# Triangular inverses with products on half the blocks, and another order of work in a mixer's first head

## The reference, cut to what matters

```python
D_MODEL, SEQ, DEPTH, N_HEADS_DN, HEAD_DIM_DN, CHUNK = 1024, 512, 2, 8, 128, 64
SHORT_CONV, DW_WIDTH, D_FF = 4, 31, 2816            # one sequence, float32

def reference(x, ...):
    for l in range(DEPTH):
        x = x + 0.5 * swiglu(rmsnorm(x), w_gate, w_up, w_down)
        x = x + hybrid_mixer(rmsnorm(x), ...)
        x = x + 0.5 * swiglu(rmsnorm(x), ...)
    return rmsnorm(x, final_norm)

def hybrid_mixer(h, ...):
    qkv, g_out, a, b, glu, gates = split(h @ w_in)
    q, k, v = split(silu(causal_depthwise_conv(qkv, taps=4)))      # 8 heads of 128
    beta, g = sigmoid(b), -exp(a_log) * softplus(a + dt_bias)
    o = gated_delta_chunked(l2norm(q) * 128 ** -0.5, l2norm(k), v, g, beta)
    y_a = (rmsnorm(o, head_norm) * silu(g_out)) @ w_a_out
    c = causal_depthwise_conv(val * sigmoid(gt), taps=31) + bias
    y_b = silu(rmsnorm(c)) @ w_b_out
    return (sigmoid(gate_a) * y_a + sigmoid(gate_b) * y_b) @ w_o

def gated_delta_chunked(q, k, v, g, beta):
    m = einsum(kb, k) * decay_strict                # strictly lower triangular
    sol = triangular_solve(eye + m, rhs)            # here: by the inverse of eye + m
    ...
    step: v_new = u - w @ state; o = qd @ state + attn @ v_new; state = state * eg + kd^T @ v_new
```

## Time and profile before

| | us |
|---|---|
| median of 3 runs | 2915.28 |
| lowest, highest | 2908.36, 2915.95 |
| the profiled execution, its own time | 2912.12 |
| its span, first to last instruction | 2910.3 |

### The profile page before, as it was taken

The page is one execution under the profiler, slowest core; times in us unless marked ns, Lnnn a source line. Parts: engine busy times, 40 slices in busy tenths (PEclk is TensorE's granted clock), DMA queues, the critical chain, the costliest instruction groups (busy, mean ns, idle before and its releaser), DMA issues.

```text
span 2910.3 us, 37509 instructions
## 1 busy us (share of the span) xinstructions
PE 2835.3 (97%) x13920; PEld 2365.2 (81%) x13920; DVE 1661.6 (57%) x2465; ACT 1103.3 (38%) x1650; POOL 335.4 (12%) x292
## 2 busy tenths in 40 slices
PE   7999989999999999999999999899999999999999
PEld 6888867888887888888888888688888878888887
DVE  5554346888887345554345543578788853555432
ACT  3322245555554233332322223455465532333221
POOL 1000021211222010000000001211121310200001
PEclk8999999999999999999999999999999999999999
DMA  4333386786664533333333335768867554233332
GB/s 142 101 94 96 90 126 108 108 111 118 112 117 74 110 94 94 94 102 94 96 95 100 94 92 100 128 105 105 120 108 115 116 75 105 87 100 95 94 97 68
DMA packets 479201, 296.80 MB, mean 102 GB/s; under 512 B 12181, under 2 KB 462869, under 8 KB 479093
## 3 DMA queue, kind: packets, MB, share of 16 engines
q1 hardware_dynamic: 462964, 236.63, 38.3%
q0 software_dynamic: 16128, 58.73, 10.5%
HBM read 234.51 MB, written 2.10 MB: 81 GB/s over the span
## 4 chain that ended last, share of the span: by engine, by line
PE 84%; DVE 5%; ACT 5%; DMA 3%; issue 2%; POOL 1%; SPq 0%; POOLq 0%; DVEq 0%; ACTq 0%
PE bank L428 82%; PE bank L565 2%; DMA w_lo<-raw 1%; DMA raw<-in_w_in 1%; DVE cacc L1274 1%; ACT w_hi L781 1%; ACT w_lo L783 1%; ACT NT L926 1%; ACT kd L932 0%; DVE w_lo L1048 0%; DMA prow<-in_qkv_conv_w 0%; DVE XT L1386 0%; DVE mg_lo L1512 0%; ACT thv L922 0%; DVE g_lo L1064 0%
## 5 line engine op out<-in xcount | busy, mean ns | idle before, releaser
L781 ACT ACTIVATE w_hi<-raw 128x1024 fp32r<-128x1024 f32 x448 | 472.3, 1057 | 635.1 <-PE bank L428 614.7
L1048 DVE TENSOR_TENSOR w_lo<-raw,w_hi 128x1024 fp32r<-128x1024 f32 x336 | 412.9, 1229 | 507.6 <-ACT w_hi L781 507.6
L428 PE MATMUL bank<-h_hi,w_hi 128*128 128x512 f32 x1504 | 591.0, 393 | 13.2 <-DVE h_lo L1073 6.0
L428 PE MATMUL bank<-h_lo,w_hi 128*128 128x512 f32 x1504 | 588.5, 391 | 0.0
L428 PE MATMUL bank<-h_hi,w_lo 128*128 128x512 f32 x1504 | 588.4, 391 | 0.0
L1274 DVE SCALAR_TENSOR_TENSOR cacc<-c_raw,ncol,cacc 128x512 f32<-128x512 f32 x464 | 381.1, 821 | 7.8
L428 PE MATMUL bank<-g_lo,w_hi 128*128 128x512 f32 x928 | 380.9, 410 | 0.0
L428 PE MATMUL bank<-g_hi,w_lo 128*128 128x512 f32 x928 | 379.8, 409 | 0.0
L428 PE MATMUL bank<-g_hi,w_hi 128*128 128x512 f32 x928 | 376.5, 406 | 0.0
L428 PEld LDWEIGHTS bank<-h_hi,w_hi 128*128 128x128 f32 x1504 | 284.3, 189 | 74.7 <-issue 10.8
L428 PEld LDWEIGHTS bank<-h_hi,w_lo 128*128 128x128 f32 x1504 | 284.2, 189 | 59.8
(11 more groups left out here) (245 smaller groups left out, 3713.2 us busy)
## 6 DMA issues: line engine op xcount, KB each, us to landing
raw<-in_w_in SPq DMA_DIRECT2D x128, 512.0 KB, 8.7
w_lo<-raw POOLq DMA_DIRECT2D x112, 512.0 KB, 7.0
raw<-in_ffn_w_gate SPq DMA_DIRECT2D x88, 512.0 KB, 3.8
raw<-in_ffn_w_up SPq DMA_DIRECT2D x88, 512.0 KB, 3.8
raw<-in_ffn_w_down SPq DMA_DIRECT2D x64, 512.0 KB, 3.9
raw<-in_ffn_w_down SPq DMA_DIRECT2D x32, 384.0 KB, 3.4
raw<-in_w_a_out SPq DMA_DIRECT2D x16, 512.0 KB, 5.1
raw<-in_w_b_out SPq DMA_DIRECT2D x16, 512.0 KB, 4.1
```

The source lines that it names most:

```text
L428: return nc.tensor.matmul(o, a, b, start=start, stop=stop, **kw)
L781: nc.scalar.activation(w_hi[c % SLOTS][:, :], raw[c % SLOTS][:, :], ACT.Copy).then_inc(hi_done, 1)
L1048: tt(w_lo[c % SLOTS][:, :], raw[c % SLOTS][:, :], w_hi[c % SLOTS][:, :].bitcast(F32), ALU.subtract).then_inc(lo_v, 1)
```

## The change

Three parts.

The inverse: a level's off-diagonal blocks lie in odd rows' blocks and even columns' blocks only. X is now packed: ScalarE copies the odd columns' blocks (XO) and the even ones (XE) of all four chunks out of bank 0, each 256 columns in place of 512. GpSimd packs the odd blocks of NT for each level (n0 to n5, 256 elements). Each small product then serves two chunks at once: y and xy are two products in place of four, the transposes between levels two in place of four. A half-wide product on VectorE (YD) with a mask of diagonal blocks takes the place of the masked copy; xy accumulates into the even blocks of bank 0, which holds X itself; one full copy (XF) and one full transpose (xtf, XTF) follow the last level. On ScalarE dense_steps(0), (1) and (2) now follow halves(1), (3) and (5), and the negatives of two units are moved between levels. On GpSimd deci comes ahead of mean_root, and n0 and n1 too. VectorE has the same lists, with two taps behind the last level.

Round 0: norm_stats after 6 half-stages in place of 12, norm_spread after 13 in place of 18; norm_factor ahead of the work on wab; lo of unit 3, wab_lo and hnh behind scale(0); the k taps before the wait for ScalarE's first exponents, and those ahead of w_hi of unit 2's successor; the sums of g after half-stage 63 and the exponents behind unit 4.

Residues of the first four mixer units by VectorE instead of ScalarE and DMA.

```diff
-PE_ORDER = "H H gr H H kt kk H kq H so H H x2t vt H H y0 fb H H xy0".split()
+PE_ORDER = "H H gr H H kt kk H kq H so H H x2t vt H H xt0 y0 fb H H xy0".split()
 for _l in range(1, LEVELS):
-    PE_ORDER += f"H H H H xt{_l - 1} y{_l} H H H xy{_l}".split()
-PE_ORDER += "H H vn0 H H os0".split()
+    PE_ORDER += ("H H H " if _l < LEVELS - 1 else "H H H H ").split() + f"xt{_l} y{_l} H H H xy{_l}".split()
+PE_ORDER += "H H H xtf H H H vn0 H H os0".split()
...
                     elif name[0] == "y":
                         lv = int(name[1:])
-                        ac("X2")
-                        ac("kd")
-                        if lv:
-                            ve(f"x{lv - 1}")
-                        each(bank[1], NT, X, name)
+                        ac(f"XE{lv}")
+                        pe.wait_ge(po_dn.sem, po_dn.after(rn, f"n{lv}"))
+                        t, at = NO[lv]
+                        for q in range(2):
+                            m = mm(bank[1][:, q * P:q * P + P], t[:, (at * 2 + q) * P:(at * 2 + q + 1) * P], X[:, (2 + q) * P:(3 + q) * P])
+                        m.then_inc(*pe_dn.step(name))
...
                 def xy(lv, rn):
-                    pe.wait_ge(ac_dn.sem, ac_dn.after(rn, f"Y{lv}"))
-                    if lv < LEVELS - 1:
-                        each(bank[2], XT, Y, f"xy{lv}")
-                    else:
-                        each(bank[2], Y, XT, f"xy{lv}")
+                    pe.wait_ge(ac_dn.sem, ac_dn.after(rn, f"XT{lv}"))
+                    pe.wait_ge(ve_dn.sem, ve_dn.after(rn, f"yd{lv}"))
+                    even = alternate(bank[0], lv, 0)
+                    nb = P // (2 << lv)
+                    for q in range(2):
+                        m = mm(even[:, q * nb:q * nb + nb, :], XT[:, q * P:q * P + P], YD[:, q * P:q * P + P].rearrange("p (b s) -> p b s", s=2 << lv),
+                               start=False, stop=True, skip_group_check=True)
+                    m.then_inc(*pe_dn.step(f"xy{lv}"))
...
                             if rn is None:
-                                if s == HALVES:
+                                if s == HALVES // 2:
                                     norm_stats(l * 3 + 1, 2)
-                                elif s == HALVES + HALVES // 2:
+                                elif s == HALVES + 1:
                                     norm_spread(l * 4 + 1, 3)
...
+                                elif s == 5 * HALVES + 3:
+                                    ab_sums()
...
+                    def halves(lv):
+
+                        pe_(f"xy{lv - 1}" if lv else "x2t")
+                        nc.scalar.activation(packed(X, 0, lv), alternate(bank[0], lv, 1), ACT.Copy).then_inc(*ac_dn.step(f"XO{lv}"))
+                        nc.scalar.activation(packed(X, 1, lv), alternate(bank[0], lv, 0), ACT.Copy).then_inc(*ac_dn.step(f"XE{lv}"))
+
+                    def turned(lv):
+
+                        pe_(f"xt{lv}")
+                        nc.scalar.activation(XT[:, 0:2 * P], bank[2][:, 0:2 * P], ACT.Copy).then_inc(*ac_dn.step(f"XT{lv}"))
...
+                    halves(0)
+                    turned(0)
+                    halves(1)
                     dense_steps(0, *dense)
...
+                    turned(1)
+                    hi(Rd, c0 + 4)
+                    halves(2)
+                    turned(2)
+                    negative(c0 + 4)
+                    halves(3)
+                    squares(0, 1)
+                    dense_steps(1, *dense)
+                    turned(3)
+                    hi(Rd, c0 + 5)
+                    halves(4)
+                    turned(4)
+                    negative(c0 + 5)
+                    halves(5)
+                    squares(2, 3)
+                    dense_steps(2, *dense)
+                    turned(5)
+                    hi(Rd, c0 + 6)
...
+                    pe_(f"xy{LEVELS - 1}")
+                    nc.scalar.activation(X[:, :], bank[0][:, :], ACT.Copy).then_inc(*ac_dn.step("XF"))
+                    pe_("xtf")
+                    nc.scalar.activation(XT[:, :], bank[3][:, :], ACT.Copy).then_inc(*ac_dn.step("XTF"))
...
-                            pe_(f"xy{lv}")
-                            t, at = (X, I_LV + lv) if lv < LEVELS - 1 else (XT, I_LASTT)
-                            dve.sem_inc(xy_seen, 1)
-                            nc.vector.copy_predicated(chunked(t), where(at), chunked(bank[2])).then_inc(*ve_dn.step(f"x{lv}"))
+                            pe_(f"y{lv}")
+                            tt(YD[:, :].rearrange("p (q c) -> p q c", q=2), bank[1][:, 0:2 * P].rearrange("p (q c) -> p q c", q=2),
+                               cst[:, I_LV + lv:I_LV + lv + 1, :].broadcast_to([P, 2, P]), ALU.mult).then_inc(*ve_dn.step(f"yd{lv}"))
                         put(behind[lv])
...
                         ve("skE")
                         tt(sm[:, 3, :], sm[:, 0, :], pw[:, 1, :], ALU.pow).then_inc(*po_dn.step("rk"))
+                        ac("decT")
+                        if before:
+                            pool.wait_ge(pe_tl.sem, pe_tl.after(rn - 1, "so"))
+                        tt(chunked(attn), chunked(dec), each_chunk(I_INCL), ALU.mult).then_inc(*po_dn.step("deci"))
+                        ve("NT")
+                        odd_columns(0)
+                        odd_columns(1)
                         if before:
                             mean_root(rn - 1)
-                        ac("decT")
-                        tt(chunked(attn), chunked(dec), each_chunk(I_INCL), ALU.mult).then_inc(*po_dn.step("deci"))
                         lo(Rd, G, c0 + 3)
                         ac("eg")
                         ve("qT")
                         tt(qd[:, :], qd[:, :], qT[:, :], ALU.mult).then_inc(*po_dn.step("qd"))
+                        ve("vT")
+                        pool.wait_ge(po_dn.sem, po_dn.after(rn, "deci"))
+                        for lv in range(2, LEVELS):
+                            odd_columns(lv)
```

More of the change, by code:

```diff
@@ L149, in trunk @@
         hb = [*hf, *sqb]
+        YD = sb("YD", [2 * P])
         arena = place[0]
@@ L949, in head @@
-                    hi(Rd, c0 + 4, residue=True)
-                    for t in range(1, 5):
-                        if rn is None and t == 3:
-                            ab_first()
-                        if rn is not None:
-                            for lv in ((1, 2), (3, 4), (5,), ())[t - 1]:
-                                level(lv)
-                        if gates:
-                            c_square(2 * t - 2)
-                            if t < 4:
-                                c_square(2 * t - 1)
-                        dense_steps(t, *dense)
-                        if rn is None and t == 1:
-                            norm_hi(l, range(4, KT))
-                        hi(Rd, c0 + t + 4, residue=not gates or t < 4)
@@ new lines, in head @@
+                    act.wait_ge(ve_ds.sem, ve_ds.after(rn, "v3"))
+                    nc.scalar.activation(thv[:, :], va[:, :], ACT.Tanh).then_inc(*ac_dn.step("thv"))
+                    act.wait_ge(po_tl.sem, po_tl.after(rn - 1, "sum"))
+                    pe_("kt")
+                    for c in range(NC):
+                        a = nc.scalar.activation(NT[:, c * P:c * P + P], bank[1][:, c * P:c * P + P], ACT.Square, accum_out=ksum[:, c:c + 1])
+                    a.then_inc(*ac_dn.step("ksq"))
@@ new lines, in head @@
+                    ve("dmin")
+                    nc.scalar.activation(dec[:, :], dec[:, :], ACT.Exp).then_inc(*ac_dn.step("decT"))
+                    nc.scalar.activation(qd[:, :], bank[0][:, :], ACT.Exp).then_inc(*ac_dn.step("eg"))
+                    for c in range(NC):
+                        a = nc.scalar.activation(kd[:, c * P:c * P + P], bank[1][:, c * P:c * P + P], ACT.Copy, scale=hs[:, HS_KD, c:c + 1])
+                    a.then_inc(*ac_dn.step("kd"))
+                    act.wait_ge(ve_tl.sem, ve_tl.after(rn - 1, "og"))
@@ L970, in head @@
+                    negative(c0 + 6)
+                    squares(4, 5)
+                    dense_steps(3, *dense)
+                    hi(Rd, c0 + 7, residue=True)
+                    squares(6)
+                    dense_steps(4, *dense)
+                    hi(Rd, c0 + 8, residue=not gates)
+                    nc.scalar.activation(NT[:, :], qT[:, :], ACT.Square, scale=float(np.sqrt(P * EPS))).then_inc(*ac_dn.step("qsq"))
+                    squares(KT - 1)
                     if not gates:
-                        pe_(f"xy{LEVELS - 1}", rd - 1)
@@ L1115, in ffn @@
                     for c in range(12):
-                        if not (i == 1 and c >= 8) or (w == 1 and not end and c < 11):
+                        if not (i == 1 and c >= 8) or (not end and c < 10 + w):
                             lo(l * R_LAYER + (r_d + 3 * i), None, c + 4)
```

207 lines of the change are left out of this document (105 added, 102 removed).

## The result

| | before | changed |
|---|---|---|
| median us | 2915.61 | 3003.60 |
| lowest to highest | 2908.36 to 2919.0 (4 runs) | 2999.8 to 3006.74 (4 runs) |
| ratio, 95% interval | | 1.0314 (1.0298 to 1.0331) |
| mean granted clock | 0.988 | 0.969 |

The forecast was 3006 with a range of 2945 to 3078. First the page of the changed kernel: busy time of each engine and share of the span, to be read against the earlier trace rows.

The account below looks back on a forecast made before the run. TensorE, 97% busy, was the bound, VectorE second; after the change VectorE's list would need longer than TensorE in most levels. From the profiled 2912.1 us, 83 + 2 + 5 + 24 - 20 = +94 gave 3006 us, range 2945 to 3078.

Parts of the forecast that it names:

- (b): Levels 0, 2, 4: VectorE's convolution taps wait 2.7 us from YD's end for ScalarE's tap behind XY.
- Part 1: The inverse's products two by two: TensorE's queue 5.3 us a head shorter, but VectorE's list, walked per level, sets the time.
- the walk's two versions: YD0 to YD5 in a head: 28.7 us with the waits for ScalarE's taps, 22.1 without them.
- (e): Granted clock: one 3.4 us stretch at half speed a head, 1.7 us each for 14 heads, +24 us.
- (a): Ahead of XY0: GpSimd's new copies slow VectorE, so YD0 ends 1.5 us later, at 577.5.
- Copies at 1.28: GpSimd's copies each costing VectorE 1.28 us: +10 us a head; with half clock after every gap 3084 us, chance 0.08.
- (c): End of the levels: 3.8 us from XY5 to vn0, making +6.9 us a head, +83 for 12 middle heads.
- largely swallowed: A half-clock stretch after XY0 or XY3 is mostly hidden by VectorE's queue; after XY5 nothing hides it.
- the wait for va: TensorE in the changed profile would wait about 1 us on va.
- (d): First and last delta heads of a layer: +1 us each first head, +2.5 each last, +2 and +5 in all.
- The rounds' part: First dense head: reordering and VectorE's residues remove TensorE's waits (hs, sg, w_lo, abT, norm), -20 us.
- TensorE stays the bound: Rival: VectorE catches up and both the 85 us and the 20 us are gained, 2807 us, chance 0.04.

Follow-up runs that it names:

- run 1: The kernel before with only round 0's new order and VectorE's residues, the inverse as before: 2891.47 us.
- run 2: The changed kernel with ScalarE's dense_steps(0), (1), (2) ahead of halves(1), (3), (5): 2910.75 us.
- run 4: The changed kernel with each of GpSimd's six packed copies made twice, first into a spare tile nobody reads: 3004.64 us.
- run 10: Run 9 with the product qd on VectorE behind YD5 in place of GpSimd, and one tap moved to the third chunk: 2824.60 us.
- 9: Run 7 with GpSimd's mean_root ahead of deci and of the first two packed copies: 2841.54 us.
- run 11: Run 10 with GpSimd's n0 ahead of the root and n1 behind deci: 2824.47 us.
- run 12: The changed kernel with only VectorE's lists levelled, no level above six pieces, ScalarE's order left as is: 2858.60 us.
- run 8: The changed kernel with GpSimd's deci product waiting for VectorE's x2T: 3003.46 us.
- run 7: The changed kernel with ScalarE's taps ahead of the halves, VectorE's lists levelled, and GpSimd's deci waiting for x2T: 2831.45 us.

## Why the prediction was right, step by step

| step | forecast | measured |
|---|---|---|
| round 0 and residues | -20 | -22 (run 1) |
| inverse, all | +114 | +112 (run 1 against changed) |
| a middle head, clock included | +6.9 + 1.7 = 8.6 us | +8.3 us in layer 0 (mean of six heads, 56.46 to 64.74), +7.5 in layer 1 (57.25 to 64.73) |
| YD0 later | +1.5 | +1.1 |
| wait (b), YD's end to q1 | 2.7 | 2.62 |
| levels 0 to 4, YD to YD, of the head shown | 6.1, 4.0, 6.4, 5.1, 7.1 | 5.96, 4.93, 6.91, 4.93, 7.02 |
| YD0 to YD5 | 28.7 | 29.75 (mean of 12 heads 29.3) |
| the same without (b) | 22.1 | 23.1 (run 2; mean of 12 heads 24.1) |
| XY5 to vn0 | 3.8 | 5.31 |
| first delta head of a layer, clock included | +1.0 + 1.7 = 2.7 us | +3.8 us (57.97 to 61.76) |
| last delta head of a layer, x2T to vn0 | +2.5 | +2.65 (37.55 to 40.20) |

**The sum came out by code and mostly by size.** Part 1's queue walk found the bound (VectorE's list between two YD, with the wait for ScalarE in it) and put the levels right within 0.2 us where TensorE doesn't hold VectorE up as well (0, 3 and 4). Run 2 takes that wait away and gives back 6.7 us from YD0 to YD5 in the heads shown and 5.3 in the mean, where the walk's two versions differ by 6.6. That the sum is 2 us off is partly luck, since errors in its terms cancel: in the head shown YD0 costs 0.4 us less than forecast and levels 0, 3 and 4 together 0.4 less, but level 1, level 2 and the way from XY5 to vn0 come to 2.9 more, for which (e) had 1.7.

**(a) was nearly the right size, for a reason only half seen.** YD0 is 7.99 us behind x2T; x0 was 6.93, so +1.06 where +1.5 was taken. Nearly all of it is at one tap, 1.66 us in the earlier trace rows and 2.65 now. GpSimd's qd stands beside it in both kernels, the copies n2 to n5 only now. From x2T to attn it is 4.02 us (569.67 to 573.69) and was 3.97, and in run 4, which makes n0 and n1 twice, 4.12: n0 and n1, two of the three copies that were priced, cost next to nothing there. What the prediction overlooked is that deci was already a cost in the kernel before, only at another place. VectorE's timeline before, x2T and the two late taps:

```profile
568.69 0.73 DVE L1386 COPY_PREDICATED XT<-cst,NT 128x512 f32<-128x512 int32 x1 [0.17 <-ACT kd L932]
...
570.20 2.54 DVE L1274 SCALAR_TENSOR_TENSOR cacc<-c_raw,ncol,cacc 128x512 f32<-128x512 f32 x2
```

Two taps took 2.54 beside deci then, 1.54 now; x2T takes 1.44 in place of 0.73. VectorE loses nothing by the swap, but x2T is on TensorE's path, and its wait there went from 10.3 to 18.6 us in all. The larger share of GpSimd's cost at that tap is qd's, which the kernel before has too: 1.3 us a head by run 10 against 9. "Copies at 1.28" as an upper bound was too pessimistic: with twice the copies (run 4) YD0 comes no later.

**(b), the main step, holds.** From the end of YD it is 2.62 us to q1 and to v1, but 3.17 to k1: in level 1 of this head VectorE waited for TensorE, and XY2 starts 0.77 us behind YD2's end (588.97 to 589.74), where the walk had 0.06. The term that was off inside it is ScalarE's half-wide copy: 0.36 taken, 0.28 from one to the next (578.94, 579.22). The product of two was 0.43 to 0.44 (578.22 to the next at 578.65) where 0.41 was taken.

**(c) and (e): the clock costs more than one stretch a head.** Level 1 came 0.9 above the walk, level 2 0.5, and the way from XY5 to vn0 1.5. Half clock stands in three places of this head: 0.57 in 571 to 575, behind a wait of 1.05 us for x2T; 0.61 in 584 to 588, behind the wait of 1.84 ahead of XY1; and 0.59 in 608 to 612, behind 2.45. The first is swallowed by the wait for YD0. In the second, VectorE idles 1.09 us ahead of YD2 for TensorE; the prediction had no stretch there. Behind XY5 nothing swallows it, as forecast. A clock of 0.92 over the head, with only the levels of 1.2 and 2.4 GHz, is 16% of the time at the lower, some 10 us where 3.4 were taken.

The heads are not all alike. In the next one (x2T at 634.78) the same wait for x2T leaves the clock at full, and half clock stands behind XY0, XY3 and XY5 instead:

```profile
636.00:640.00 4.00, 3.60 (x24) 3.10 (x25) 3.93 (x8) 1.04 (x3) 4.00 (x5) 1.00 0.38 109
...
660.00:664.00 4.00, 3.96 (x15) 3.40 (x16) 3.82 (x6) 0.75 (x3) 0.00 (x0) 0.58 0.25 66
```

Its levels are 6.48, 3.75, 6.49, 4.93 and 7.52: a stretch behind XY0 costs level 0 0.5 us, one behind XY3 costs level 3 nothing, as "largely swallowed" had it. The gaps themselves were smaller than the walk's (1.40 and 1.84 us ahead of XY0 and XY1, not about 3 and 2 to 3). Ahead of XY0 this is because TensorE arrives late itself, by x2T's 0.7 us and the stretch at half clock. There is a gap of 0.81 ahead of XY4 too, and the wait for va that was foretold isn't there.

**(d), and the 112 us counted through.** From hs copy to hs copy, the changed kernel's profiled execution against run 1's: the twelve middle heads are 95.0 us longer in all (7.9 each), the two first delta heads 6.9, what follows from each layer's last hs copy 9.4, and what stands ahead of the first 1.4; together 112.7. The forecast had 83 and 20 of the clock's 24 for the middle heads, so these were put some 8 us too high, and the rest, 10 in the forecast, came to 18. Where the line between heads is drawn matters: in every head but a layer's first the hs copy now stands 1.3 us earlier (8.21 us ahead of x2T in place of 6.87), as two taps ahead of it have moved, so 2.7 of the 9.4 belong to the first heads. From x2T to vn0 a first head is 4.2 us longer (37.43 to 41.65), its levels taking 30.2 us where the walk had 28.7, and a last head 2.65 (forecast 2.5). What is left was not followed.

**The rounds' part.** -22 against -20; of its terms abT gained 2.4 us in the changed kernel and 1.7 in run 1 where 0.8 was taken, and hs, sg and w_lo went as forecast.

**The rivals.** "TensorE stays the bound" at 2807 was rightly unlikely for this kernel, but it is nearly what runs 10 and 11 reach (2824.5) with VectorE's list and ScalarE's order mended: of the 5.3 us a head that TensorE was spared, 56.5 - 52.5 = 4.0 arrive. The remaining waits are for GpSimd's copy n0 in run 10 (16.9 us in all) and for YD in run 11 (22.5). One sum of the prediction doesn't fit its text: the ends of the terms, +34 to +172, give 2946 to 3084, not 2945 to 3078.

What stays open: how much of the 112 us is the clock alone. It can't be varied by itself, and a run that removes waits removes both; the shares given for it above are readings of one trace.

## What to carry to other kernels

Where one engine is 97% busy and another is second by a few microseconds, cost a saving for the first per stage, against the second one's written list between two hand-overs, not against its mean load. A wait put into an in-order queue costs its length only where nothing independent stands ahead of it: first look for work to put there (run 12, 145 us), then for a way to remove it (run 2, 93 us). And test two repairs together before adding their gains: 33.5 and 93 made 94.

## What the hardware showed that was not expected

**GpSimd beside VectorE.** An operation of VectorE with two inputs in SBUF can lose up to what GpSimd's instruction beside it takes. v's product lost 1.54 us beside a qd of 1.54; a tap takes 0.75 alone, 1.66 beside qd, 2.04 to 2.72 with qd and copies beside it in a middle head, 1.35 with the copies alone (run 10); the predicated copy 0.73 alone, 1.44 beside a deci of 1.28. Even the copy of 48 elements takes 0.17 alone and 1.28 beside a deci of 1.60 (run 8). GpSimd is slowed in its turn (deci 1.28, 1.60 and 1.82 us in the changed kernel, run 7 and run 11), so an estimate from either one's undisturbed time is too low. VectorE doing qd itself costs 0.69 us and gives back 1.3.

The Trainium skill (SBUF — State Buffer, Who interferes with whom) says that a VectorE instruction with two SBUF inputs contends with one of GpSimd that reads SBUF, and that one with at most one SBUF input doesn't, outside VectorE's two-port modes. The first half agrees with the taps here, and so does the second with attn's product, whose second input is in PSUM and which stays at 0.67 to 0.69 in the timelines read. The slowed copy of 48 elements has a single SBUF input, so by this rule it would have to run in such a mode; no trace here shows the mode.

**The clock does not follow the length of one gap.** Behind a wait of 1.05 us (571.16) the next stretch has 0.57, in the next head behind 1.06 us (636.27) 1.00; behind one of 1.84 us (584.19) it has 0.61, behind one of 2.25 us (596.02) 1.00, and in the earlier trace rows 1.90 left it at 1.00. Six waits of 0.8 to 2.5 us in a head go with a mean of 0.93 over six heads, where it was 1.00; removing most of them (run 10) brought 1.00 back.
